# Where the fourth weight block of a projection pair is loaded, and when, in a one-core Trainium2 encoder layer

## The reference, cut to what matters

```python
proj = x @ w_in[i]                     # (4096 x 1024) @ (1024 x 3328)
aq, ak, av, ag, bq, bk, bv, bg = jnp.split(proj, split_at, axis=-1)
# chunked attention (A), sliding-window attention with sinks (B), SiLU gates, output projection, LayerNorm
```

## Time and profile before

| | |
|---|---|
| median of 3 runs | 2608.16 us |
| lowest, highest | 2604.04, 2610.0 us |
| the profiled execution's own time | 2606.84 us |
| span of its trace | 2605.1 us, mean granted TensorE clock 0.98 |
| instructions | 37929 |

### The profile page before, as it was taken

How to read it: one execution, slowest core, us unless ns; L and a number is a source line. 1 busy time by engine, 2 the same in 40 slices (tenths; PEclk the granted TensorE clock), 3 DMA queues, 4 the chain that set the end, 5 groups by cost and what they waited for, 6 DMA issues and landing times. The chain is left out here.

```text
span 2605.1 us, 37929 instructions
## 1 busy us (share of the span) xinstructions
PE 2480.7 (95%) x13620; PEld 2161.2 (83%) x13620; DVE 1695.0 (65%) x3215; ACT 1193.5 (46%) x2438; POOL 379.3 (15%) x226
## 2 busy tenths in 40 slices
PE   6999999999999999989999999968999999999997
PEld 4778887888789778989999998966888888888886
DVE  7887788768886888378888886863424333333333
ACT  4343443343333434278888887962222222222322
POOL 0100000000000000000000000123343434444341
PEclk9999999999999999999999998989999999999998
DMA  3645265435544554565666547965544545354540
GB/s 133 199 151 157 105 207 161 140 124 192 165 121 157 183 158 108 185 211 184 210 209 195 179 128 250 317 181 159 114 120 112 121 110 123 108 127 113 126 113 24
DMA packets 352693, 402.52 MB, mean 155 GB/s; under 512 B 83856, under 2 KB 257056, under 8 KB 346784
## 3 DMA queue, kind: packets, MB, share of 16 engines
q1 hardware_dynamic: 348544, 390.34, 50.8%
q0 software_dynamic: 4000, 10.25, 1.2%
HBM read 265.50 MB, written 136.07 MB: 154 GB/s over the span
## 5 line engine op out<-in xcount | busy, mean ns | idle before, releaser
L1638 DVE TENSOR_TENSOR y_lo<-y_raw,y_hi 128x1024 fp32r<-128x1024 f32 x32 | 39.2, 1226 | 396.2 <-ACT y_hi L1138 396.2
L980 ACT ACTIVATE wop_hi<-w_raw 128x512 fp32r<-128x512 f32 x288 | 174.1, 622 | 179.1 <-DVE w_raw L1279 153.6
L925 POOL DMA_DIRECT2D yb_d<-y_b x32 | 20.4, 637 | 1616.8 <-ACT y_b L1180 1591.0
L1538 DVE CUSTOM_DVE_ANT_0 prob<-psum,bias 128x640 f32<-128x640 f32 (+4 forms) x256 | 199.3, 778 | 73.6 <-issue 73.0
L1109 ACT ACTIVATE prob<-prob,small 128x640 f32<-128x640 f32 (+4 forms) x256 | 203.9, 797 | 60.7 <-DVE small L1538 60.7
L1740 PE MATMUL psum<-xs_lo_b,wop_hi 128*128 128x512 f32 x528 | 207.9, 394 | 0.0
L1740 PE MATMUL psum<-xt_hi,wop_hi 128*128 128x512 f32 x480 | 190.0, 396 | 16.7 <-issue 7.2
L1740 PE MATMUL psum<-wo_hi,y_hi 128*128 128x512 f32 x512 | 202.8, 396 | 1.3 <-DVE wo_lo L1633 1.3
L1554 DVE TENSOR_TENSOR pt_lo<-psum,pt_hi 128x640 fp32r<-128x640 f32 (+4 forms) x256 | 199.2, 778 | 4.2 <-ACT pt_hi L1118 4.2
L1740 PE MATMUL psum<-wo_hi,y_lo 128*128 128x512 f32 x512 | 200.2, 391 | 0.0
L1740 PE MATMUL psum<-wo_lo,y_hi 128*128 128x512 f32 x512 | 200.1, 391 | 0.0
(11 more groups left out here) (210 smaller groups left out, 6465.6 us busy)
## 6 DMA issues: line engine op xcount, KB each, us to landing
w_raw<-in_w_blocks SPq DMA_DIRECT2D x168, 256.0 KB, 3.9
qk_d<-stage_out SPq DMA_DIRECT2D x72, 512.0 KB, 4.1
v_d<-stage_out SPq DMA_DIRECT2D x64, 320.0 KB, 2.4
bq_d<-stage_out SPq DMA_DIRECT2D x64, 256.0 KB, 4.0
g_d<-stage_out SPq DMA_DIRECT2D x64, 256.0 KB, 2.3
ya_d<-y_a SPq DMA_DIRECT2D x128, 128.0 KB, 2.5
bq<-bq_d SPq DMA_DIRECT2D x32, 512.0 KB, 5.8
y_two<-ya_d SPq DMA_DIRECT2D x32, 512.0 KB, 4.6
```

What stands on the lines that cost most here:

```text
L925: pool.dma_start(yb_d[pair * P:pair * P + 4 * HEAD, t0:t0 + 4 * CHUNK].rearrange("(h d) t -> d h t", d=HEAD), y_b[:, d % 2, :, :]).then_in ...
L980: act.activation(wop_hi[:, n % W_RING, :, :], w_raw[:, i, :, :], ACT.Copy).then_inc(w_hi_done, 1)
L1538: dve.tensor_tensor_reduce(out=prob[:, r, NBW - n * P:NBW].rearrange("p (a b) -> p a b", a=2), in0=psum[:, 0:2, 0:n * P // 2], in1=bias[:, ...
L1638: dve.tensor_tensor(y_lo[:, :, :], y_raw[:, s, :, :], y_hi[:, :, :].bitcast(f32), ALU.subtract).then_inc(y_split, 1)
```

## The change

The fourth block (a22) of the pairs a = 2, 4, 6 and 8 no longer goes to `w_raw[:, 6]` but to the first quarter of X22's raw memory. The odd pairs, and pair 0, still use `w_raw[:, 6]`. Because the two places alternate, the load of a22 of pair a waits for the split of (a-2, 6) in place of (a-1, 6), and not for the mixes of the pair before; it is issued in slot (a-2, 6), right behind blocks 0 to 2 of its pair, and no longer in slot (a-1, 2). For a = 2 it waits until the x operands of the group are split. Pair 1's fourth block is issued where it was. Engines read a22 at its new place. Numbers of instructions, bytes and DMAs stay as they are.

```diff
+        def a22(a):
+            return x_raw_b[:, 1, 0, :].rearrange("p (k m) -> p k m", m=P) if a in (2, 4, 6, 8) else w_raw[:, 6, :, :]
 ...
             def load_w(g, a, b):
                 i = (0, 1, 3, 6)[b]
                 n = BK * g + a
+                if b == 3 and a > 1:
+                    sp.wait_ge(x_split, 14 * (g + 1))
+                    if a > 2:
+                        sp.wait_ge(w_split, ring(g, a - 2, 6) + 1)
+                    sp.dma_start(a22(a), w_blocks[PAIRS[a][1] // P + 1, 1]).then_inc(w_loaded[3], 16)
+                    return
                 if a > 0:
                     sp.wait_ge(w_split, ring(g, a - 1, i) + 1)
 ...
-                    if i == 2 and a + 1 < BK:
-                        load_w(g, a + 1, 3)
+                    if (a, i) == (0, 2):
+                        load_w(g, 1, 3)
                     if i == 6 and a < BK - 1:
-                        for b in range(3 if a < BK - 2 else 2):
+                        for b in range(4 if a < BK - 2 else 2):
                             load_w(g, a + 2, b)
 ...
-                act.activation(wop_hi[:, n % W_RING, :, :], w_raw[:, i, :, :], ACT.Copy).then_inc(w_hi_done, 1)
+                act.activation(wop_hi[:, n % W_RING, :, :], a22(a) if i == 6 else w_raw[:, i, :, :], ACT.Copy).then_inc(w_hi_done, 1)
 ...
-                    dst, x0, x1, how = a21, a21, a22, ALU.add
+                    dst, x0, x1, how = a21, a21, a22(a), ALU.add
 ...
             def w_lo(n):
-                _, _, i = ring_at(n)
+                _, a, i = ring_at(n)
+                raw = a22(a) if i == 6 else w_raw[:, i, :, :]
```

More of the change, by code:

```diff
@@ L1260, in mix_weights @@
                 n = BK * g + a
-                a11, a12, s2, a21, s3, s4, a22 = (w_raw[:, i, :, :] for i in range(7))
+                a11, a12, s2, a21, s3, s4 = (w_raw[:, i, :, :] for i in range(6))
                 if op == 0:
@@ L1281, in w_lo @@
             def w_lo(n):
-                _, _, i = ring_at(n)
+                _, a, i = ring_at(n)
+                raw = a22(a) if i == 6 else w_raw[:, i, :, :]
                 dve.wait_ge(w_hi_done, n + 1)
-                dve.tensor_tensor(wop_lo[:, n % W_RING, :, :], w_raw[:, i, :, :], wop_hi[:, n % W_RING, :, :].bitcast(f32),
+                dve.tensor_tensor(wop_lo[:, n % W_RING, :, :], raw, wop_hi[:, n % W_RING, :, :].bitcast(f32),
                                   ALU.subtract).then_inc(w_split, 1)
```

## The result

The changed kernel takes 2583.08 us, the median of 3 runs (2578.45 to 2585.09), against 2608.16: ratio 0.9898, 95% interval 0.9879 to 0.9918. The profiled execution took 2585.09 us, with a span of 2583.3.

The account below looks back on a forecast made before the run. TensorE, busy 95%, was taken as the bound, so gains come from its stalls and half clock. Group gains and ends sum to 22.3 us: 2606.84 gives 2584.5, plus 1.3 for the run median, 2586 us; range 2580 to 2600.

Parts of the forecast that it names:

- The bound and the chain of cause: Projections: TensorE bounds, 95% busy; VectorE's waits for the fourth block, 45.3 us, lead to TensorE's `wop_lo` stalls, 23.7 us.
- Waits removed: Projections: VectorE's load waits fall from 45.3 to under 8 us, `wop_lo` from 23.7 to about 10; `vw_lo` waits go.
- The sum by groups: Projections: groups 0 to 3 gain 4.0, 2.4, 5.6 and 6.6 us, the group ends 3.7; sum 22.3 us.
- The cost of the burst: DMA burst at pair 6: the moved block delays stores by 1.2 us, of which 0.9 is charged to VectorE.
- the sentence on the other pairs: Pairs other than 5 and 6: VectorE's own lead covers the cost; groups 1 to 3 stall on `wop_lo` only at those two.
- Late next: After the change: VectorE's roped work, with store waits (1.74 us) and TensorE's lead at pair 6, thin by 1 us in groups 2, 3.
- The queue rival: Burst stores land by bytes alone, so VectorE waits longer there; only 3.7 us at group ends stay, 2604.4 us; chance 0.08.
- the slower one: Stores behind four loads land late, 7.6 us together, delaying ScalarE's `stage_out`; 7.5 us slower, 2616 us; chance 0.03.
- The half of the queue rival that had SyncE hold the block back: SyncE, held by the first of four loads, issues the fourth as late as before; counted within the 0.08 chance.

Follow-up runs that it names:

- slot 0: Changed kernel's new memory, but fourth blocks of pairs 3 to 9 (2 too in groups 1 to 3) issued in slot (a-1, 0); 27.6 us faster than before, ratio 0.9897.
- slot 1: Changed kernel's new memory, but fourth blocks of pairs 3 to 9 (2 too in groups 1 to 3) issued in slot (a-1, 1); 31.0 us faster than before, ratio 0.9885.
- The second profile: A second profile of the same changed kernel, nothing altered; attention A starts at 1083.2 us and nothing is lost behind the projections.
- the old slot and the new waits: Changed kernel's new memory and weaker waits, but the fourth block issued in the old slot (a-1, 2); ratio 1.0006 to the kernel before.

## Why the prediction was right, point by point

**The bound and the chain of cause** (fourth block, op 1, `wop_lo`, TensorE) are shown: undoing the early issue brings all waits back, pairs 5 and 6 carry 20 us, pair 9 the group ends. One name is wrong: the leftovers that VectorE works through behind the wait at 400 us are those of pair 3, rotated during pair 4, which is not roped itself.

**Waits removed.** "Falls from 45.3 to under 8 us" was 7.1; "`wop_lo` to about 10" was 10.7. I had named pair 1 alone as the rest; in fact 5.5 us of it, in six places, are op 0 of pairs 4 and 8 waiting for a block of the first three. With the fourth block out of the burst, in slots 0 and 1, only two such waits are left in each kernel, 1.7 us in all with slot 0 and 2.0 with slot 1; that the fourth lengthened the burst is the likely reason, from one execution each. No half clock is left behind the products of pair 6, near 693 and 963 us, as foretold.

**The sum by groups**, in the product stretches:

| | forecast | measured | remark |
|---|---|---|---|
| group 0 | 4.0 | 4.4 | stall at (6, 1) 1.9, forecast 2.9 |
| group 1 | 2.4 | 2.8 | |
| group 2 | 5.6 | 4.8 | 6.4 without a new half clock |
| group 3 | 6.6 | 9.2 | 7.6 without a half clock of before |
| group ends | 3.7 | 4.9 | |
| to the start of A | 22.3 | 26.3 | with 0.3 at the start |

The sum was 4.0 us too small to the start of A, and 3.4 of them are one thing: a stall's idle time is not all it costs. At the group ends it is 1.2 us more than the stall rows. In group 1 the last pair product's last matmul and the first value matmul start 1.64 us apart before and 0.23 after, 1.42 us for a row of 1.26; the matmuls behind a stall take up the rest. It is so in the pairs too: without half clock, groups 1, 2 and 3 gained 2.8, 4.7 and 5.9 us for stall rows of 2.4, 3.9 and 4.9. The half clock that moved between the two executions, as told below, took 1.6 us from group 2 and gave 1.6 to group 3, so it cancels in the sum.

That group 0 came near its 4.0 is partly luck. The stall of 3.0 us at 136 shrank to 0.6 and the half clock behind it went, as foretold, but the stall near 102 grew from 1.7 to 3.1 us, and a stretch of half clock of 6.6 us, which before doesn't have, stands behind it. So is part of the agreement of the time: in the profiled execution 26.3 us of gain to the start of A met 4.6 of loss behind it. The second profile gained 25.0 and lost nothing.

**The cost of the burst.** I took 1.2 us on the stores and 0.9 on VectorE at pair 6, and one more load there measured 0.7 to 0.9. The text failed in the sentence on the other pairs, whose cover, "VectorE's own lead", I used as if it were free. It held for the change, but at pair 4 a load uses twice as much of it, and one more load there costs time. VectorE's waits for `stage_out` in the pairs (L1359 and L1377) went from 25.3 to 31.7 us, 1.6 us per group. The growth that I had put at about 1 us per group was that of ScalarE's waits for stores before it fills `stage_out` in the pairs: 63.1 to 65.7 us, 0.7 per group.

**"Late next"** was to be the thin lead at pair 6. At product (6, 1) it measures 0.6, 2.3 and 1.0 us in groups 1 to 3. By my sum 2.5, 0.9 and 0.6 were left over: the total is right here, and group 1 was not the safe one. The second profile has 0.15, 1.8 and 1.0, so that even the total is partly luck.

**The queue rival** had the early arrival lost at the next store. It is out, and so is the slower one: even a fifth load per pair still leaves 18 us of gain. Late stores are not only in the burst at pair 6, as the text on the slower rival has it: in group 1 of the kernel before, stores issued at 350.4 and 352.2 landed after 5.5 and 5.8 us too. The half of the queue rival that had SyncE hold the block back is what happens in the run with the old slot and the new waits, and it is a real trap of this kernel.

## What to carry to other kernels

Read a late load back to what stands ahead of it in its queue's order, not only to its own semaphore: here the semaphore was met, and the load stood behind stores that waited for the very engine that needed it. Keep the lead of a helper engine as an account along the stage; a wait taken out early in the account pays for later ones too, and a load issued one slot sooner was as good here as one three slots sooner. A buffer that another stage leaves idle is worth it when it lets a load be issued ahead of such a wait.

## What the runs showed of the hardware

**The same stall, with and without half clock.** TensorE stands 2.39 to 2.42 us at the fifth product of groups 1 to 3 in every one of the 14 traces. Behind it, the kernel before:

```profile
314.50:317.80 3.30, 3.13 (x8) 2.48 (x9) 3.30 (x5) 2.60 (x5) 0.00 (x0) 0.50 0.00 0
581.40:584.70 3.30, 3.30 (x15) 2.70 (x16) 3.30 (x5) 2.37 (x5) 0.00 (x0) 1.00 0.00 0
850.40:853.70 3.30, 3.30 (x9) 2.59 (x8) 3.30 (x6) 1.19 (x3) 0.00 (x0) 0.50 0.00 0
```

and after it the changed one, first behind its stall of 3.1 us in group 0:

```profile
101.70:108.30 6.60, 5.76 (x14) 4.53 (x15) 4.94 (x11) 0.00 (x0) 0.83 (x1) 0.50 0.82 235
309.90:313.10 3.20, 3.20 (x9) 2.44 (x8) 3.20 (x4) 1.75 (x4) 0.00 (x0) 0.50 0.00 0
572.70:576.00 3.30, 3.30 (x10) 2.56 (x9) 3.30 (x5) 1.29 (x3) 0.00 (x0) 0.50 0.00 0
834.00:837.30 3.30, 3.30 (x15) 2.71 (x16) 3.30 (x5) 2.35 (x5) 0.00 (x0) 1.00 0.00 0
```

The columns are those of the earlier trace rows: third from the right is the granted clock, 0.50 for 1.2 GHz and 1.00 for 2.4 GHz. The stall is the same to 0.02 us in these two traces, and it is followed by half clock in one group and not in another, at 9 or 10 matmuls for 15. In the 14 traces half clock follows in 31 of the 42 places, in all three groups of some executions and in none of one. Each such stretch costs 1.6 to 1.7 us, so that two traces may differ by 5 us (three of them, an estimate) at this place alone. Whoever reads a gain from two traces should count these out; here they moved 1.6 us out of group 2's gain and into group 3's.

**Issuing takes longer behind a two-part store.** One `w_raw` load's issue takes 0.33 us at least and 0.41 in the median, and 0.38 behind three loads in the changed kernel (the row at 382.09). Close behind the two-part store of bq it took 1.31 in slot 1 and 1.30 in the old slot, the same 256 KB. Why is not shown.
